# Product-key experts on one core: a gate map written by scatters of per-expert totals in place of one built by TensorE, and v loaded in pairs of tiles

## What is computed

```
q = einsum('nd,dhk->nhk', x, w_q)                  # 8 heads, two halves of 128
s1, s2 = scores of the halves against 128 sub-keys each
v1, i1 = top_k(s1, 16); v2, i2 = top_k(s2, 16)
sc, sel = top_k(v1[..., :, None] + v2[..., None, :], 16)   # per head
eidx = (i1 * 128 + i2) at sel                      # 8 x 16 = 128 experts a token
gate = softmax(sc)
a    = x . u_emb[eidx];  coef = gelu(a) * gate
out  = sum over the 128 of coef * v_emb[eidx]
```

## Time and profile before

| | us |
|---|---|
| median of 3 runs | 1928.85 (1923.22 to 1933.78) |
| the profiled execution | 1916.39 |
| its span | 1914.5 |
| granted TensorE clock, mean | 0.971 |
| DMA moved | 337.63 MB, 176 GB/s |

### The profile page before, as it was taken

How to read it: one execution, slowest core, us unless ns; L and a number is a source line. 1 busy time by engine, 2 the same in 40 slices (tenths; PEclk the granted TensorE clock), 3 DMA queues, 4 the chain that set the end, 5 groups by cost and what they waited for, 6 DMA issues and landing times. The chain is left out here.

```text
span 1914.5 us, 24469 instructions
## 1 busy us (share of the span) xinstructions
PE 1815.5 (95%) x8991; PEld 1491.0 (78%) x8991; DVE 1184.6 (62%) x2275; ACT 668.0 (35%) x1004; POOL 579.2 (30%) x422
## 2 busy tenths in 40 slices
PE   5999999988999689999999999999999999999997
PEld 4877867866788467888888888888888888888885
DVE  3259945542799977888622222232467888888885
ACT  4333203342332223666532222222343333333332
POOL 3644300010544550000000000000177777777820
PEclk9999996988999889999999999999999999999998
DMA  4322110051232333789884444455488999999992
GB/s 136 100 66 56 45 31 1 1 176 55 83 105 78 89 100 109 177 210 235 209 222 148 148 140 146 151 148 188 138 294 269 362 364 372 376 362 372 366 340 88
DMA packets 241690, 337.63 MB, mean 176 GB/s; under 512 B 119856, under 2 KB 178608, under 8 KB 241472
## 3 DMA queue, kind: packets, MB, share of 16 engines
q1 hardware_dynamic: 219088, 269.60, 45.6%
q0 software_dynamic: 22528, 67.19, 9.7%
HBM read 282.19 MB, written 54.53 MB: 176 GB/s over the span
## 5 line engine op out<-in xcount | busy, mean ns | idle before, releaser
L344 PE MATMUL psum<-x_hi,ts_hi_u 128*128 128x512 f32 x1024 | 405.9, 396 | 22.1 <-DVE ts_lo_u L1157 18.9
L346 PE MATMUL psum<-x_hi,ts_lo_u 128*128 128x512 f32 x1024 | 402.4, 393 | 0.0
L345 PE MATMUL psum<-x_lo,ts_hi_u 128*128 128x512 f32 x1024 | 402.2, 393 | 0.0
L1919 POOL DMA_INDIRECT sparse_rows<-in_peer_v,sparse_v_row x128 | 161.5, 1262 | 752.1 <-PE psum L346 662.2
L1157 DVE TENSOR_TENSOR ts_lo_u<-ts_raw_u,ts_hi_u 128x1024 fp32r<-128x1024 f32 x117 | 157.9, 1350 | 370.5 <-ACT ts_hi_u L1152 370.1
L345 PE MATMUL psum<-v_lo,c_hi 128*128 128x512 f32 x768 | 298.8, 389 | 0.0
L346 PE MATMUL psum<-v_hi,c_lo 128*128 128x512 f32 x768 | 298.8, 389 | 0.0
L344 PE MATMUL psum<-v_hi,c_hi 128*128 128x512 f32 x768 | 298.8, 389 | 0.0
L1819 ACT ACTIVATE v_hi<-v_raw 128x1024 fp32r<-128x1024 f32 x128 | 135.8, 1061 | 316.0 <-PE psum L346 276.1
L1185 ACT ACTIVATE ut_out_u<-psum 128x512 f32<-128x512 f32 x128 | 76.6, 598 | 484.1 <-PE psum L346 373.9
L344 PEld LDWEIGHTS psum<-x_hi,ts_hi_u 128*128 128x128 f32 x1024 | 194.6, 190 | 63.5 <-DVE ts_lo_u L1157 19.3
(11 more groups left out here) (231 smaller groups left out, 2636.3 us busy)
## 6 DMA issues: line engine op xcount, KB each, us to landing
ts_raw_u<-in_peer_u SPq DMA_DIRECT2D x128, 512.0 KB, 3.8
v_raw<-in_peer_v SPq DMA_DIRECT2D x128, 512.0 KB
gate_map<-gate_stage SPq DMA_DIRECT2D x48, 512.0 KB, 5.7
up_acts<-ut_out_u SPq DMA_DIRECT2D x96, 192.0 KB, 1.9
act_in<-up_acts SPq DMA_DIRECT2D x96, 192.0 KB
gate_in<-gate_map SPq DMA_DIRECT2D x96, 192.0 KB
raw_in<-in_w_in SPq DMA_DIRECT2D x56, 256.0 KB, 2.8
ts_raw_wq<-in_peer_wq SPq DMA_DIRECT2D x16, 512.0 KB, 4.1
```

The lines of the kernel that those rows point to most:

```text
L344: nc.tensor.matmul(out, l_hi, r_hi, start=first, stop=False)
L345: nc.tensor.matmul(out, l_hi, r_lo, start=False, stop=False)
L346: return nc.tensor.matmul(out, l_lo, r_hi, start=False, stop=last)
L1919: nc.gpsimd.indirect_dma_start(dn.rows[:, r], None, v_rows, bass.IndirectOffsetOnAxis(sparse["v_row"][:, j:j + 1], 0)).then_inc(row_in[r], 16)
```

## The change

The gate map is no longer built by matmuls. In route, SP fills `gate_map` with zeros (32 stores). For each dense token and each of its 128 picks VectorE computes the sum of the gates of all picks with the same expert (`total_gate`, one instruction per block and pick, 384 in all, ten a tile), and GpSimd writes these totals to their places in `gate_map`, 128 values of 4 bytes an instruction (`scatter_gate`, 384 indirect DMAs). Picks of one token that name the same expert write the same total. The transposes in route are gone. No coefficients stay in SBUF: all 128 down tiles load activations and gates. The tiles come in their natural order. v is loaded two tiles at a time through a ring of eight; the loads for the first eight tiles and the waits for all scatters stand in SP's list at tile 102 of 104, and ScalarE splits the first four tiles ahead of the last GELU.

```diff
-RESIDENT = 32
+ZERO_COLS = 1536
+ZERO_STORES = P * DENSE // ZERO_COLS
...
         nc.scalar.activation(self.out[:, slot], self.bank[slot], ACT.Gelu).then_inc(self.bank_read, 1)
...
-        if n < NKEYS - RESIDENT:
-            sp.dma_start(acts_d[n], self.out[:, slot, 0:DENSE]).then_inc(self.stored[slot], 16)
+        sp.dma_start(acts_d[n], self.out[:, slot, 0:DENSE]).then_inc(self.stored[slot], 16)
...
+            def store_zeros(x):
+                sp.dma_start(gates_d.rearrange("e p f -> e (p f)")[:, x * ZERO_COLS:(x + 1) * ZERO_COLS], zeros[:]).then_inc(zeroed, 16)
+
             sp.dma_start(sub_keys[:], io["sub_keys"]).then_inc(keys_in, 16)
+            sp.wait_ge(zeros_done, 1)
             for j in range(2, G + 2):
                 load_q(j)
...
+                for x in range(n * ZERO_STORES // STEPS, (n + 1) * ZERO_STORES // STEPS):
+                    store_zeros(x)
...
-                pe.wait_ge(picked_done, b + 1)
-                flat = "p h k -> p (h k)"
-                bank = psum[:, 2 + b % 4]
-                nc.tensor.transpose(bank[:, 0:P], picked[:, b % 2, 0].rearrange(flat), ident[:])
-                nc.tensor.transpose(bank[:, P:2 * P], picked[:, b % 2, 1].rearrange(flat), ident[:])
-                nc.tensor.transpose(bank[:, 2 * P:3 * P], gates[:, b].rearrange(flat), ident[:]).then_inc(turned, 1)
...
+            def addresses(b):
+
+                i1, i2 = (picked[:, b % 2, t].rearrange("p h k -> p (h k)") for t in range(2))
...
+                number = expert[:, b] if b < DENSE_BLOCKS else sparse_expert[:]
+                nc.vector.scalar_tensor_tensor(out=number, in0=i2, scalar=float(P), in1=i1,
+                                               op0=ALU.mult, op1=ALU.add).then_inc(placed, 1)
+                dve.wait_ge(placed, b + 1)
+                if b < DENSE_BLOCKS:
+                    nc.vector.tensor_scalar(places["gate_at"][:, b], number, float(DENSE), frame[:, b:b + 1],
+                                            ALU.mult, ALU.add)
...
+            nc.gpsimd.memset(zeros[:], 0.0).then_inc(zeros_done, 1)
...
     RING = 4
+    RAW = 8
     GATHERED = 8
...
-        self.resident = sb("resident_coef", [P, RESIDENT, DENSE], c=c)
-        self.up_gate = sb("up_gate", [P, 2, DENSE], c=c)
-        self.v_raw = sb("v_raw", [P, self.RING, D], c=c)
+        self.v_raw = sb("v_raw", [P, self.RAW, D], c=c)
...
+    TOTALS = 10
...
+            def total_gate(m, b, j):
+
+                if m >= 2:
+                    dve.wait_ge(totalled, m - 1)
+                nc.vector.scalar_tensor_tensor(out=dn.same[:, j % 2], in0=expert[:, b], scalar=expert[:, b, j:j + 1],
+                                               in1=gates[:, b].rearrange("p h k -> p (h k)"), op0=ALU.is_equal,
+                                               op1=ALU.mult, accum_out=dn.total[:, b, j:j + 1]).then_inc(totalled, 1)
...
             ut.split_lo(nc.vector, dve, R + 1, 1)
-            dve.wait_ge(spread, 4 + 2 * PARTS)
             for n in range(TILES):
-                if n < STEPS:
-                    one_hots(n, n % 2)
                 if n + 2 < TILES:
                     ut.split_lo(nc.vector, dve, n + (R + 2), n % 2)
-                if n >= FIRST_KEPT:
-                    keep(n)
-                if n >= LEAD and (n - LEAD) % 2:
-                    low((n - LEAD) // 2)
+                for m in range(n * TOTALS, min((n + 1) * TOTALS, DENSE_BLOCKS * SLOTS)):
+                    total_gate(m, *place(m))
+            for e in range(EARLY):
+                product(e)
+                low(e)
...
-            with pe.Fori(1, STEPS // 2) as it:
-                for par in range(2):
-                    ut.product(nc, pe, x_hi, x_lo, it * 2 + (R + par + 1), 1 - par, False)
-                    rows(it * 2 + par, par, False)
...
+            with pe.Fori(0, TILES // 2) as it:
                 for par in range(2):
-                    ut.product(nc, pe, x_hi, x_lo, it * 2 + (R + par + 1), 1 - par, False)
-            ut.product(nc, pe, x_hi, x_lo, R + TILES - 1, 1, False)
-            pe.wait_ge(staged, STEPS * banks)
+                    ut.product(nc, pe, x_hi, x_lo, it * 2 + (R + par), par, False)
...
+            for n in range(TILES):
+                if n == TILES - 1:
+                    for e in range(EARLY):
+                        split_down(e)
                 finish_up(n)
                 next_split(n)
...
+            def load_v_pair(e):
+
+                i = e % RAW
+                if e >= RAW:
+                    sp.wait_ge(v_lo_done, e - RAW + 2)
+                sp.dma_start(dn.v_raw[:, i:i + 2], io["peer_v"][:, e:e + 2]).then_inc(v_in[i // 2], 16)
...
             for n in range(TILES):
                 if n + 2 < TILES:
                     ut.load(sp, io["peer_u"], R + n + 2, n % 2, R + n + 2, False)
...
+                if n == TILES - 2:
+                    for e in range(0, RAW, 2):
+                        load_v_pair(e)
+                    for b in range(DENSE_BLOCKS):
+                        sp.wait_ge(scattered[b], 16 * SLOTS)
+                    for i in range(2):
+                        sp.wait_ge(ut.stored[i], 16 * (RAW // 2))
+                    for e in range(RAW):
+                        load_coef(e)
                 ut.store(sp, acts_d, acts_s, R + n, n % 2)
             sp.wait_ge(ut.product_done, NKEYS)
...
+            def scatter_gate(b, j):
+
+                nc.gpsimd.indirect_dma_start(
+                    gate_cells, bass.IndirectOffsetOnAxis(places["gate_at"][:, b, j:j + 1], 0),
+                    dn.total[:, b, j:j + 1], None).then_inc(scattered[b], 16)
+
+            pool.wait_ge(zeroed, 16 * ZERO_STORES)
+            for m in range(DENSE_BLOCKS * SLOTS):
+                b, j = place(m)
+                h, k = divmod(j, PEER_TOPK)
+                if h and k == 0:
+                    pool.wait_ge(scattered[b], 16 * PEER_TOPK * h)
+                pool.wait_ge(totalled, m + 1)
+                scatter_gate(b, j)
             pool.wait_ge(ut.product_done, NKEYS)
```

More of the change, by code:

```diff
@@ L1182, in gelu @@
         if n >= 2:
-            act.wait_ge(self.stored[slot], 16 * min(n // 2, (NKEYS - RESIDENT) // 2))
+            act.wait_ge(self.stored[slot], 16 * (n // 2))
             act.wait_ge(self.sparse_stored[slot], 16 * (n // 2))
@@ L1480, in _ @@
                 sums(b - 1)
+                addresses(b - 1)
                 low_u(sel_up + SEL * b + 1)
@@ L1485, in _ @@
             low_u(ROUTE_TILES)
-            sparse_places()
+            addresses(NB - 1)
         @block.gpsimd
@@ L1692, in weigh @@
                 dve.wait_ge(picked_in[body % 2], 16 * BODY * (body // 2 + 1))
-                nc.vector.tensor_tensor(dn.weight[:, cols], dn.picked[:, cols], sparse["gate"][:, cols], ALU.mult).then_inc(weighed, 1)
+                nc.vector.tensor_tensor(dn.weight[:, cols], dn.picked[:, cols],
+                                        gates[:, NB - 1].rearrange("p h k -> p (h k)")[:, cols], ALU.mult).then_inc(weighed, 1)
                 dve.wait_ge(weighed, body + 1)
@@ L1728, in _ @@
             for e in range(EARLY, NKEYS):
-                if e >= RESIDENT:
-                    product(e)
+                product(e)
                 low(e)
@@ L1745, in _ @@
         def _(pe):
-            def rows(n, par, first):
-                pe.wait_ge(hot_done, n + 1)
-                for r in range(STEP):
-                    q, at = divmod(r, BANKROWS)
-                    if at == 0 and not first:
-                        pe.wait_ge(staged, n * banks - (banks - 1 - q))
-                    out = psum[:, q, at * P:(at + 1) * P]
-                    for x in range(PARTS):
-                        last = nc.tensor.matmul(out, gm.one1[:, par, r], gm.val2[:, par, x, r], start=x == 0,
-                                                stop=x == PARTS - 1)
-                    if at == BANKROWS - 1:
-                        last.then_inc(mapped, 1)
             def down(e, i, first, final):
@@ L1793, in _ @@
         def _(act):
-            def copy_rows(n, at, par):
-                for q in range(banks):
-                    act.wait_ge(mapped, n * banks + (q + 1))
-                    nc.scalar.activation(
-                        gm.stage[:, par, :, bass.ds(at + q * BANKROWS, BANKROWS)].rearrange("p i n -> p n i"),
-                        psum[:, q, :].rearrange("p (n i) -> p n i", i=NKEYS), ACT.Copy).then_inc(staged, 1)
             def finish_up(n):
-                if n >= FIRST_KEPT + 2:
-                    act.wait_ge(kept, kept_at(n) - 1)
                 ut.gelu(nc, act, R + n, n % 2)
@@ L1903, in _ @@
             sp.dma_start(g_final[:], io["norm_final"][0:1, :].broadcast_to([P, D])).then_inc(g_final_in, 16)
-            for e in range(RING, NKEYS):
-                load_v(e)
-                if e >= RESIDENT:
-                    load_coef(e)
+            for i in range(2):
+                sp.wait_ge(ut.stored[i], 16 * (NKEYS // 2))
```

(4 more changed lines are left out.)

275 lines of the change are left out of this document (68 added, 207 removed).

## The result

The kernel became slower: 2204.05 us in the median of four runs (2166.8 to 2216.98) against 1926.14 before (1923.22 to 1933.78); the ratio is 1.132 with a 95% interval of 1.118 to 1.146. It goes by the two fastest runs of the changed kernel (2166.8 and 2195.65), since the two others lie over 1.5% above its fastest and count as slow. The forecast was 1862. The profiled execution took 2166.8 us with a span of 2164.9, that is 250 us more than the 1916.4 of before.

What follows compares the result with a forecast made beforehand. The prediction took TensorE as the bound; -67.2 - 13 + 1 + 13 = -66.2 us took the profiled 1916.4 to 1850.2, and the same difference from the median 1928.85 gave 1862 us. The range was 1843 to 1915.

Steps and rivals of the forecast that it cites:

- a scatter stream that ends by 1300 costs nothing: Up stage, GpSimd's scatters: free if ended by 1300 us, a pace of 1.457 us; each 0.1 us beyond costs 38 us.
- Hidden.: Scatters on the DMA engines: 60 to 150 us of each engine in 550, beside a share of 0.47, costs nothing.
- DMA side: Scatter packets: 49152 of 4 bytes, 3072 an engine, at 0.02 to 0.05 us each, taken as hidden.
- The pace: GpSimd's scatters in the up stage: 1.44 us each, from about 740.5 to 1293 us.
- Rival (c): GpSimd's scatters blocked for all of VectorE's busy time: down stage starts +62 us later, 1991 us; chance 0.04.
- Rival (e): 4-byte writes cost more than reads and DMA engines bound: at 0.12 us a packet, 2008 us; chance 0.05.
- Gate matmuls, -67.2: Up tiles: without the gate map's matmuls, 24 steps each save 2.80 us of TensorE, -67.2 us.
- Route, -13 + 1: Route: removed transposes and TensorE stops give -13 us (0 to -16); added zero stores and VectorE operations +1.
- My layout of VectorE's queue: Route on VectorE: hits, sums, low halves and addresses laid out again leave two short waits, 1.5 and 1.7 us.
- the zero stores: Route: 32 stores of 768 KB on SP's queue, in a term of +1 us with bounds 0 and +8.
- Hand-over, +13: From up to down stage: later v and coefficient loads leave TensorE an 11 us gap; +13 us, bounds +5 and +18.
- Down stage, 0: Down stage: coefficient loads for every tile and v in pairs change nothing; 0 us, bounds -2 and +6.

Runs made afterwards that it cites:

- e1: Changed kernel with all 384 scatters and SP's wait for them left out, gate map left zero: 1863.01 us.
- e3: Changed kernel with each scatter writing 128 rows of 512 bytes to another tensor instead of 128 cells of 4 bytes, map left zero: 2195.93 us.
- e2: Changed kernel with each scatter turned into a 4-byte gather from the same addresses, map left zero: 2223.08 us.
- e6: Changed kernel with each scatter waiting until the one issued four before it has landed: 2232.60 us.
- e8: Changed kernel with the scatters replaced by 384 plain transfers from GpSimd's queue to another tensor, map left zero: 2020.11 us.
- e5: Changed kernel with four gate totals a tile on VectorE instead of ten: 1962.20 us, ratio 1.019.
- e9: Changed kernel with a blank write by GpSimd behind each scatter, of 32, 256, 512 and 1024 columns for 96 scatters each: 2046.47 us.
- e11: Changed kernel without scatters, SP's queue writing each total as a plain transfer to another tensor, map left zero: 2173.95 us.
- base: The changed kernel without its scatters, gate map left zero, the same run as e1: 1863.01 us.
- kernel after: The changed kernel as profiled, with all scatters, against the kernel before the change: 2166.8 us profiled, median 2204.05, ratio 1.132.
- e12: Changed kernel without scatters, raw v loaded in single 512 KB transfers instead of pairs, map left zero: 1865.85 us, ratio 0.971.
- e10: Changed kernel with GpSimd pausing by blank writes behind each group of 8 scatters, later of 16: 1994.01 us.
- e13: Changed kernel with blank writes of 256, 192, 128 and 64 columns behind each scatter, for 96 scatters each: 1953.69 us.
- e16: Changed kernel, whole computation, with a 64-column blank write behind each scatter and the hits multiplied by VectorE: 1887.77 us, ratio 0.986 to the kernel before.
- e18: Changed kernel, whole computation, with a 96-column blank write behind each scatter and nothing else: 1903.51 us, ratio 0.993 to the kernel before.
- e7: Changed kernel with each scatter writing 64 frames instead of 128, half of the map's entries left out: 2236.05 us.

## Why the prediction was wrong

**The step that failed** is the rule under which the scatters were costed: "a scatter stream that ends by 1300 costs nothing", and with it the "Hidden." at the end of "DMA side". The term was put at nothing because the stream would end in time and the DMA engines had time left. What a dense stream would do to the other engines had no term. It cost 304 us (e1).

The runs show that this price hangs neither on bytes (e3) nor on direction (e2) nor on unfinished transfers (e6) nor on packets as such (e8), but on how densely GpSimd issues index-driven transfers. Held up were streams with an undisturbed period of 1.26 us (after, e5) and 1.38 (e9); free were 1.41 and more, means of 1.55 and more. That the same queue did no harm before was in the rows I had read: 1.68 us a gather, because GpSimd there waits for rows and for VectorE. I used that number for how late the stream might be, and didn't ask what a denser one would do to others.

**DMA side: too dear, and harmless.** The forecast was 3072 packets an engine and 60 to 150 us of each. The trace has 32 packets a scatter, and GpSimd's queue in 760 to 1319 (packets, MB, share of 16 engines):

```profile
q0 software_dynamic: 12224, 0.22, 1.6%
```

That is 9 us of each engine. The 0.16 us a row packet from which the price was derived stands in no row. So by their records the DMA engines did hide the scatters; the harm came another way.

**The pace was right and didn't matter.** 1.44 us forecast, 1.459 measured, though with stalls in it; the row behind it, 0.94 + 0.30 with one wait for the VectorE operation in flight, is confirmed (0.96 + 0.30). The last scatter was issued at 1318.74, behind the 1300 that the prediction named as its limit, but the up part then still had 311 us to run. Rival (c) is out. Rival (e) has the wrong price for this form, the index-driven one; for plain transfers of 4 bytes (e8, e11) its mechanism is what happens.

**Gate matmuls, -67.2:** right. 5.44 us a tile wherever scatters don't interfere, in all tiles of the base but the last.

**Route, -13 + 1:** wrong by 15 us; the base's experts start 3.1 us later than before instead of 12 earlier. Two terms. The transposes went, but GpSimd's multiply of the hits (5.9 us each) now runs beside the two low halves of every block, which take 11.03 us together for 2.35; before, that happened in one block. My layout of VectorE's queue allowed 1.2 to 2.9 us a low half. The Trainium skill (SBUF — State Buffer, section "SBUF: two separate sides") states that a VectorE operation with two SBUF inputs and a GpSimd operation that reads SBUF shut each other out for a whole instruction. For this two-input multiply the trace agrees: a low half that starts under a multiply lasts 5.5 us and ends 1.1 us after it. A scatter waits for the VectorE operation in flight, but it doesn't hold VectorE: low halves beside scatters last 1.23 us, as without. So that rule gives one wait for each operation, as I had taken for the scatters, and not the full stop of rival (c) that the prediction read into it; where it did cost something I had left it out. And the zero stores cost some 11 us, not 1, beyond my bound of 8. The two together (18.3 + 10.8 = 29) are more than the 15 us missed, so either they overlap or the transposes' -13 was too small; no run tells.

**Hand-over, +13:** right. The first coefficient's product began 16.2 us after the v loads ahead of it were issued (16.8 forecast), and TensorE stood 9.0 us (11), in the kernel after.

**Down stage, 0:** right (e12, and the full 443 matmuls in 1700 to 1800).

The sum of the rest, 1850 for the profiled execution, met the base at 1863: 15 us missed in the route, 2 won at the hand-over. All of the 304 us is the one term that I had set at nothing.

## What stays open

What fills up, if something does. It isn't the DMA engines as far as their records go (share 0.02 in a stall). It reaches several engines at once: TensorE starts its instructions 0.70 us or a multiple apart, ScalarE's GELU starts 38 us late, SP's transfers wait behind it, GpSimd isn't touched.

The nearest rival is the recording of the profile itself. Every time in this document comes with a span and a granted clock of the same execution, so it was taken while events were recorded. Every kernel with such stalls lacks update events (20% of them are recorded in the kernel after, 29% in e5, 43% in e10, 66% in e9, from 760 to 1310); in the kernels without stalls 97% or more are there (base, e13, e16 to e18). Events are also missing ahead of the first stall and in e10's free groups of 8, so the loss isn't just a result of the stalls. A path for semaphore updates or their records that scatters overrun would fit that several engines are held up while DMA packets are on time. It is not shown: no run was timed without the recording, and whether the stalls exist there isn't known.

Another rival is the fetching of instructions. The Trainium skill (Runtime: NRT & Kernel Launch, section "Instruction fetch mechanics") says that each sequencer fetches its instructions by a DMA queue of its own; starved fetches would look like this. The trace records packets of instruction queues, and they speak rather against it: in this stage the first two come after the 27th and after the 31st GELU, in the base (769.5 and 787.5 us) as in the kernel after (772.3 and 828.8), so none is due at the 29th, which was held up by 38 us; and the twelve that fall into the time of the scatters took 0.31 to 0.81 us each. Whether every fetch is recorded isn't known, and it wasn't tried.

The limit is known between 1.38 and 1.41 us of undisturbed period only with the hits moved to VectorE (e16); without that move 1.43 (e18) was shown free. Zero stores in a quieter stretch, and an earlier start of the scatters, which e16 to e18 would need at the hand-over, were not tried.

## What to carry to other kernels

Before moving work to an idle engine's queue, compare its issue rate with one that the trace shows to be harmless; a busy share and a sum of bytes don't tell it. A stream of index-driven transfers needed gaps here: 0.17 to 0.19 us of blank write behind each, or no more than 8 in a row with some 3.5 us between groups. This is shown for executions under the profiler only. And when an engine stands with "issue" as the reason inside a block that waits for nothing, look for what the engine that is *not* slowed is doing, and whether the trace still has its landing times: where they are missing, so is part of the record.

## What the runs showed of the hardware

- Index-driven transfers of 128 values from GpSimd's queue with an undisturbed period of 1.26 to 1.38 us stall the other engines after 12 to 20 us: for up to 63 us at a time (e3), up to 5 us beyond the last one. At an undisturbed period of 1.41 to 1.43 us (a mean of 1.55 to 1.56) they hold nothing up in 600 us. 64 values instead of 128 don't help (e7).
- With such dense transfers the trace loses events of semaphore updates (1630 of 8240 recorded), while the 4-byte packets that carry them are all there (8224).
- A plain transfer of 128 values of 4 bytes costs the others: u loads of 512 KB land after 11.8 us (e11, four in a tile) and 13.8 (e8, one every 0.94 us) instead of 3.7.
- A two-input multiply of 128 x 2048 on GpSimd stretches two VectorE subtractions from 2.35 to 11.03 us; a scatter doesn't stretch them (1.23 us each).
